# A two-pass SwiGLU and recurrent-mixer decoder step: the token half moved to the outside of every dense tile's matmul loop

## The reference, cut to what matters

```python
def swiglu_half(x, g, w_up, w_down):
    h = rmsnorm(x, g)
    gate, up = jnp.split(h @ w_up, 2, axis=-1)
    return x + 0.5 * ((jax.nn.silu(gate) * up) @ w_down)

def trunk(x, states, p):
    ...
    for l in range(DEPTH):
        x = swiglu_half(x, p['ffn1_norm'][l], p['ffn1_w_up'][l], p['ffn1_w_down'][l])
        y, st = mixer(rmsnorm(x, p['mix_norm'][l]), l, lb_all[l], p, tuple(s[l] for s in states))
        x = x + y
        x = swiglu_half(x, p['ffn2_norm'][l], p['ffn2_w_up'][l], p['ffn2_w_down'][l])
```

## Time and profile before

| | |
|---|---|
| runs of before | 3340.68, 3342.35, 3326.44 us, median 3340.68 |
| span of the profiled execution, first to last instruction | 3336.2 us |
| PE busy | 3164.9 us, 95% |
| POOL busy | 1630.8 us, 49% |
| DVE busy | 1376.8 us, 41% |
| ACT busy | 567.1 us, 17% |
| share of PE in the chain that ended last | 84%, of it 71 points in the dense matmuls of L353 |
| mean granted TensorE clock | 0.960 |

### The profile page before, as it was taken

One profiled execution on the slowest core, in us unless ns is written; L12 is line 12 of the kernel. 1 busy time (PEld: TensorE's weight loads), 2 busy tenths in 40 slices (PEclk: granted clock), 3 DMA queues, 4 the chain that ended last, 5 costly groups with the idle time before them and its releaser, 6 DMA issues.

```text
span 3336.2 us, 63241 instructions
## 1 busy us (share of the span) xinstructions
PE 3164.9 (95%) x23984; PEld 3057.0 (92%) x23984; DVE 1376.8 (41%) x1559; ACT 567.1 (17%) x820; POOL 1630.8 (49%) x908
## 2 busy tenths in 40 slices
PE   7999989898999999999999998989999999899998
PEld 7999989888988799999999998989888978899997
DVE  5232544535333564232542326354363244732326
ACT  2010022131231211010110101121403312110101
POOL 4555654333332255565665656533333323555555
PEclk9999999899988899999999999999999889999999
DMA  3222231131211232222222222311312112322222
GB/s 115 88 88 88 90 108 64 51 98 60 82 58 61 64 109 89 86 85 88 95 89 87 85 88 94 110 58 55 107 52 78 58 61 76 105 87 89 88 88 90
DMA packets 113138, 276.30 MB, mean 83 GB/s; under 512 B 9016, under 2 KB 52928, under 8 KB 112448
## 3 DMA queue, kind: packets, MB, share of 16 engines
q1 hardware_dynamic: 65088, 237.01, 21.6%
q10 hardware_dynamic: 47872, 36.71, 3.5%
HBM read 255.16 MB, written 18.52 MB: 82 GB/s over the span
## 4 chain that ended last, share of the span: by engine, by line
PE 84%; DVE 9%; issue 4%; ACT 1%; DMA 1%; POOL 1%; ACTq 0%; DVEq 0%; PEld 0%; POOLq 0%; PEldq 0%
PE dense L353 71%; PE SA L547 1%; PE SA L482 1%; PE SB L557 1%; PE SA L561 1%; PE SA L468 1%; PE SA L534 1%; DVE rows L981 1%; DVE sst L1191 1%; DVE tmp L1178 1%; DMA X<-x_keep 1%; POOL Wl L333 1%; PE SA L411 1%; DVE vblk L1184 0%; PE SA L537 0%
## 5 line engine op out<-in xcount | busy, mean ns | idle before, releaser
L331 POOL TENSOR_SCALAR Wh<-raw 128x1024 fp32r<-128x1024 f32 x452 | 490.4, 1085 | 1648.0 <-PEq L358 1638.8
L333 POOL TENSOR_TENSOR Wl<-raw,Wh 128x1024 fp32r<-128x1024 f32 x452 | 1140.2, 2523 | 37.7
L353 PE MATMUL dense<-Hh,Wh 128*128 128x272 f32 x3872 | 841.0, 299 | 49.6 <-DVE Hl L890 20.1
L353 PE MATMUL dense<-Hh,Wl 128*128 128x272 f32 x3872 | 820.3, 294 | 0.0
L353 PE MATMUL dense<-Hl,Wh 128*128 128x272 f32 x3872 | 819.6, 294 | 0.0
L353 PEld LDWEIGHTS dense<-Hh,Wh 128*128 128x128 f32 x3872 | 630.9, 195 | 63.0 <-DVE Hl L890 22.4
L353 PEld LDWEIGHTS dense<-Hl,Wh 128*128 128x128 f32 x3872 | 630.0, 195 | 0.0
L353 PEld LDWEIGHTS dense<-Hh,Wl 128*128 128x128 f32 x3872 | 625.4, 195 | 0.0
L353 PE MATMUL dense<-Mh,Wh 128*128 128x272 f32 x1408 | 293.2, 289 | 8.9 <-POOLq L335 8.9
L353 PE MATMUL dense<-Ah,Wh 128*128 128x272 f32 x1408 | 292.5, 289 | 6.8 <-DVE Al L925 4.2
L353 PE MATMUL dense<-Ml,Wh 128*128 128x272 f32 x1408 | 293.7, 289 | 0.0
(11 more groups left out here) (316 smaller groups left out, 3005.8 us busy)
## 6 DMA issues: line engine op xcount, KB each, us to landing
raw<-wst SPq DMA_DIRECT2D x452, 512.0 KB, 3.2
x_keep<-X ACTq DMA_DIRECT2D x2, 2176.0 KB, 7.8
X<-x_keep ACTq DMA_DIRECT2D x2, 2176.0 KB, 10.3
sst<-st_h ACTq DMA_DIRECT2D x8, 512.0 KB, 4.1
s_h<-sst ACTq DMA_DIRECT2D x8, 512.0 KB, 3.1
sst<-st_c ACTq DMA_DIRECT2D x8, 512.0 KB, 3.9
s_c<-sst ACTq DMA_DIRECT2D x8, 512.0 KB, 3.1
X<-xT ACTq DMA_DIRECT2D x4, 544.0 KB, 7.6
```

What stands on the lines that cost most here:

```text
L331: pool.tensor_scalar(Wh[:, j, :], raw[:, j, :], 1.0, 0.0, ALU.mult, ALU.add).then_inc(glink, 1)
L333: pool.tensor_tensor(Wl[:, j, :], raw[:, j, :], f32(Wh[:, j, :]), ALU.subtract).then_inc(glink, 1)
L353: mm = pe.matmul(dps[slot][:, a, 0:HALF], w[:, ring, w0:w0 + 128], x[:, k, a * HALF:(a + 1) * HALF], start=(k == 0 and n == 0), stop=(k == ...
```

## The change

In `dense` the loop over the token half `a` moves from the inside to the outside. Before, each weight block and pass was used for half 0 and then half 1. Now all blocks and passes run for tokens 0 to 271, and then all again for tokens 272 to 543. The waits for the blocks of `first` are made in half 0 only. The wait for `tile_done` and the raise of `w_used` stand behind block 0 of half 0. In a woven tile each part does both halves of its own blocks. The number of matmuls, their operands and what each bank accumulates in which order of k and pass stay as they were; no other function changes. Line numbers behind L344 move by one, so L353 is L354 in the changed kernel.

```diff
-                for k in range(nk) if part is None else range(part * nk // 2, (part + 1) * nk // 2):
-                    if first is not None:
-                        pe.wait_ge(first[0], first[1] + (k + 1))
-                    w0 = (k0 + k) * 128
-                    for n, (w, x) in enumerate(((Wh, hi), (Wh, lo), (Wl, hi))):
-                        for a in range(2):
+                ks = range(nk) if part is None else range(part * nk // 2, (part + 1) * nk // 2)
+                for a in range(2):
+                    for k in ks:
+                        if first is not None and a == 0:
+                            pe.wait_ge(first[0], first[1] + (k + 1))
+                        w0 = (k0 + k) * 128
+                        for n, (w, x) in enumerate(((Wh, hi), (Wh, lo), (Wl, hi))):
                             mm = pe.matmul(dps[slot][:, a, 0:HALF], w[:, ring, w0:w0 + 128],
                                            x[:, k, a * HALF:(a + 1) * HALF],
                                            start=(k == 0 and n == 0), stop=(k == nk - 1 and n == 2))
-                    if k == 0 and k0 == 0:
-                        pe.wait_ge(tile_done, ONE + t)
-                        pe.sem_inc(w_used, 1)
+                        if k == 0 and k0 == 0 and a == 0:
+                            pe.wait_ge(tile_done, ONE + t)
+                            pe.sem_inc(w_used, 1)
```

## The result

The changed kernel takes 3389.12 us (3383.59 to 3403.93, four runs) where the kernel before takes 3336.39 us in the same session: a ratio of 1.0167, interval 1.0135 to 1.02. The change makes it slower by 1.7%, about 53 us. The profiled run of after took 3403.93 us, 15 us above its median; its span is 3402.2 us, 66 us above that of before.

What follows compares the result with a forecast made beforehand. PE's dense matmuls were taken to bound the kernel. Stalls of 39.8 us plus clock drops of 19.8 made 59.6 us, put on the median of 3340.7: 3400 us, 1.8% slower, range 3365 to 3440.

Steps and rivals of the forecast that it cites:

- the clock term: Behind 13 new PE gaps: 9 drops to half clock at 2.2 us each, 19.8 us; bounds 0 and 39.
- `w_out`: Its 2 first tiles: some 2.4 us lost before block 6 go into the later wait for X, net 0.
- The stalls of the down tiles: First down tiles wait for their last block: 8 blocks, 2.34 us, 8 times, 18.7; 6 blocks, 1.9 us, 4 times, 7.5.
- The mixer's first tile: 21 matmuls move behind block 7, at the low clock: 4.2 us, twice, 8.4 us.
- The very first tile: Start of the kernel, block 7 late: at least 2.6 us, taken as 2.6.
- Layer 1's first tile: Start of layer 1: all 21 matmuls move behind block 7, 2.6 us.
- The early-ready first tiles: 6 branch tiles and 2 second-SwiGLU-block first tiles: last block ready sooner than 21 matmuls take, 0.
- stalls-only rival: Tiles waiting for blocks stall, without clock drops behind the gaps: 3381 us, chance 0.20.
- The wait for the tile before: nothing, by a hair: PE's `tile_done` wait behind block 0: three queued matmuls instead of 6 just cover it, 0 us.
- the bubble rival: A bubble in each tile at the `tile_done` wait: 20 to 40 us more, 3420 to 3440, chance 0.08.
- Steady tiles: nothing: Tiles without block waits: 24 matmuls in a row to one bank cost 0, within 10 us either way.
- The two rivals with the pitch: All dense matmuls: faster pitch, 0.115 us each, 3188 us, chance 0.06; one-bank accumulation costing 5 ns each, 3506 us, 0.05.

Runs made afterwards that it cites:

- the second profile: The changed kernel run again unaltered beside the experiments, against the kernel before: 3386.01 us, ratio 1.0163, profiled span 3383.2 us.
- The filled gaps: Changed kernel plus 16 or 21 unused matmuls before the last block wait in first and fifth down tiles: 3403.55 us, 1.0221 to the kernel before.
- the later raise: Changed kernel with the `tile_done` wait and `w_used` raise behind block 1: 3375.43 us; with tiles given `first` in old order too (behind block 0), 3342.07 us.
- the half inside the block: Changed kernel with loops reordered in all tiles to block, then half, then pass: 3349.5 us, 1.005 to the kernel before.
- the interleaved tiles: Kernel before with the mixer's first two tiles interleaved and, in 6-block down stages, the second tile's block 0 before the first's last: 3333.12 us, 0.9992.

## Why the prediction was right, point by point

3400 us was predicted, 3389 came; slower, and inside the range. The effect was 53 us, over a kernel before at 3336.4 us in that session; the forecast said 59.6 over 3340.7. The stalls, two thirds of the forecast, came as computed. That the rest of the sum came near is partly luck: the clock term was too large by 8 to 11 us, two terms put at nothing made some 14, and `w_out` gave back 4.9.

- **The stalls of the down tiles held.** With 8 blocks and no drop, the first tile takes 8.42 to 8.45 us to the next one's start, where it took 5.98 to 6.03: 2.4 us more, 2.34 forecast. With 6 blocks it is 1.85 more, 1.9 forecast. The gaps are 1.97 and 2.70 us instead of 2.2 and 2.9: the two late matmuls at the tile's start take 0.17 us of the gap, which leaves the end of the tile where it was forecast. Their sum, 26.5 us, stands for the 29.
- **The mixer's first tile held:** 17.6 and 17.4 us from the first wait to the next tile's start instead of 13.2, so 4.3 each (4.2 forecast), at the low clock as assumed.
- **The very first tile held in the end:** its last block is followed by matmuls at the slow pace (0.22 us from one start to the next, 32.36 to 32.58), so the tile itself loses more, 3.4 us to the next tile's start. But before, that next tile began at the slow pace (rows 6) and now it doesn't: the third tile starts 30.3 us after the first where it started after 27.6, 2.7 us more, 2.6 forecast. Layer 1's first tile was 2.2 (2.6), in the second profile 4.0.
- **`w_out` was absorbed**, as said, with 0.64 us left of the wait for X where 1.8 were said. What the forecast left out is the stretch at 0.50 behind that wait: with the wait it went away, and the two places together gained 4.9 us where 0 was said. The early-ready first tiles lost nothing.
- **The clock was the worst-sized term.** 9 drops of 2.2 us, 19.8, were forecast. There were 7 behind the down gaps at 1.5 us each, one of them double: 9 us by the times, 12 by the trace. Of the other profiles with the same gaps the changed kernel's second had 7 too, the others 5, 5 and 3. The mean granted clock was 0.954 and 0.959 in the changed kernel's two profiles, about 0.95 forecast. A stretch lasts 3.4 us more often than 6.8, and I had taken a value between. With a stalls-only rival at 3381 and the changed kernel at 3386 and 3389, that rival is as near to the measured medians as my forecast. The filled gaps decide between them: a cost behind the gaps exists, and it is about half of the term. One reading in the forecast was wrong as well: of the new gaps, those of 2.9 and 2.7 us don't lie between the 1.83 that kept the clock and the 2.68 that may have cost it, but above. It did no harm, since they were counted as drops; in after 3 of the 4 gaps of 2.70 us and 4 of the 8 of 1.97 us had one.
- **"The wait for the tile before: nothing, by a hair" was wrong by that hair.** The restart is late by 0.01 to 0.02 us in ordinary tiles and 0.17 us in the 16 down tiles with 8 blocks that get `first`. In 8 of these the lateness lies inside the wait and costs nothing; the other 8, the fifth tiles, make 1.4 us. By the medians in the table the later raise gives back 3 to 7 us over the 394 tiles of 8 blocks; the bubble rival's 20 to 40 us didn't come.
- **"Steady tiles: nothing" was off within its own bound.** Four up tiles take 24.24 us (from 101.55, the same tile's start in after, to 125.79), 24.05 before. The mean distance of dense matmuls at full clock went from 125.32 to 125.98 ns, and 0.66 x 21216 = 14 us, the late restarts among it. With the later raise it is 125.70 ns, so some 8 us go with the order and 6 with the restarts. The forecast had allowed half a ns, 10 us, for the order. With the half inside the block the order alone made 0.78 ns. The runs don't show why.

The two rivals with the pitch are out: it neither fell to 115 ns nor rose to 130. The Trainium skill ("TensorE: Matmul & The Clock Gate", "Back-to-back issue gap") gives 272 / 2.4 + 2.5 = 116 ns for the gap of an isolated matmul of 272 columns, an estimate by its formula. No 8-block tile that ran here took under 5.97 us, 124.4 ns per matmul, so the measurement decides, and the change of bank isn't what separates them. Why it is 125 stays open, and so does what moves a tile by up to 0.06 us between kernels with the same order in it.

The terms from the traces sum to 26.6 + 8.6 + 2.7 + 2.2 = 40.1 us for the stalls (39.8 forecast), 12 for the clock, 14 for the distance of matmuls with the restarts, and -4.9 at `w_out`: 61 us. The two profiles of the changed kernel have spans 66 and 47 us above that of before, and the medians say 53 to 54. The sum can't be held closer than that: half-clock stretches that aren't behind the down gaps take from 239 to 296 us over the 13 profiles, which at 0.447 is 25 us of time between the extremes.

## What to carry to other kernels

When a tile consumes blocks as they are produced, count the work that stands behind its last wait. In such a tile keep the loop that follows the producer outermost; a half or slice moved outside it turns covered waits into gaps. Here 16 of the 474 dense tiles (12 in the down stages, the mixer's two and the first of each layer) made most of a 1.6% loss, while the others ran almost as before. Look also at what lies behind the gap: in `w_out` a shorter later wait, and the slow stretch that went with it, took the loss back and more, and in the interleaved tiles a ring of two took the gain back.

## What the runs showed of the hardware

- Three queued matmuls of 0.125 us (0.375 us) didn't quite cover a semaphore wait that ends with the old tile's last matmul: ordinary tiles restart 0.01 to 0.02 us late, those with a wait for a block right behind it 0.17 us late. Six covered it in both.
- Gaps of 1.97 us were sometimes followed by a stretch at 0.50 and sometimes not, in the same program at the same kind of place: of the 12 gaps (8 of 1.97 us, 4 of 2.70) 7 had one in each of two profiles, 5, 5 and 3 in others; with gaps of 2.15 and 2.88 us it was 2. A drop costs 1.4 to 1.5 us, and with the gap filled by matmuls that do nothing for the result none came at any of the 12 places.
- A matmul stream with the same count, operands and banks took 125.3, 126.0 or 126.1 ns each according to the order of the operands, the first of the last two with the late restarts in it. The length of one kind of tile with the same order differed between kernels by up to 0.06 us in 6 (5.989 to 6.051).
- Two executions of the same kernel spent 314 and 279 us at half clock and differed by 19 us in their spans, 17.8 of them in one stage, the middle of layer 0's mixer.
